# Two mixers in one fused kernel: VectorE's order in the triangular solve and in its setup, one identity copy cut in four, and the hg items spread 2 2 2 2 4 4 over the levels

## The reference, cut to what matters

```
p = h @ w_in                                  # 6672 columns, in weight pieces of 256
qkv, z, beta, a, hq, hf_fwd, hf_bwd, hi, hgate, gate_dn, gate_hg = split(p)
q, k, v = silu(conv5(qkv));  q, k = l2norm(q), l2norm(k)
# gated delta rule, forward and backward, 4 heads of 128:
A = strict_tril(beta * (k @ k.T) * decay);  T = inverse(I + A)
o_dn = (q k^T * decay) applied through T to beta * v
# HGRN2, forward and backward, 4 heads of 128:
logf = log_sigmoid(f) + log1p(lb * exp(-f));  kk = (1 - lb) * sigmoid(-f)
o_hg = sum over s <= t of (q_t . kk_s * exp(b_t - b_s)) * i_s,  b = cumsum(logf)
out = (sigmoid(gate_dn) * norm(o_dn) @ w1 + sigmoid(gate_hg) * norm(o_hg) @ w2) @ w_out
```

## Time and profile before

| | us |
|---|---|
| three runs | 1750.78, 1748.83, 1751.04 |
| median | 1750.78 |
| the profiled execution | 1750.08 |
| its span | 1748.3 |
| PE busy | 1655.1 (95%) |
| DVE busy | 1237.5 (71%) |
| ACT busy | 967.5 (55%) |

### The profile page before, as it was taken

The page is one execution under the profiler, slowest core; times in us unless marked ns, Lnnn a source line. Parts: engine busy times, 40 slices in busy tenths (PEclk is TensorE's granted clock), DMA queues, the critical chain, the costliest instruction groups (busy, mean ns, idle before and its releaser), DMA issues.

```text
span 1748.3 us, 30663 instructions
## 1 busy us (share of the span) xinstructions
PE 1655.1 (95%) x13206; PEld 1603.1 (92%) x13206; DVE 1237.5 (71%) x1715; ACT 967.5 (55%) x1420; POOL 0.2 (0%) x4
## 2 busy tenths in 40 slices
PE   6997899999999997899999998999999998899997
PEld 6987899999999897899999997887999998799997
DVE  6778955777747779846777747666688838688863
ACT  6564465565536663465556534347577635577752
POOL 0000000000000000000000000000000000000000
PEclk9999999999999999999999999999999999999999
DMA  6421115455454421124455552530354553054551
GB/s 256 168 97 49 49 40 181 164 197 190 172 191 138 178 73 49 49 73 169 167 195 193 178 185 90 199 120 1 120 194 173 190 193 127 25 193 173 189 193 49
DMA packets 34983, 246.11 MB, mean 141 GB/s; under 512 B 3872, under 2 KB 4256, under 8 KB 5536
## 3 DMA queue, kind: packets, MB, share of 16 engines
q1 hardware_dynamic: 34848, 244.15, 39.4%
HBM read 243.09 MB, written 1.05 MB: 140 GB/s over the span
## 4 chain that ended last, share of the span: by engine, by line
PE 80%; DVE 13%; ACT 5%; issue 1%; DMA 0%; DVEq 0%; ACTq 0%
PE PS L395 79%; DVE SA L1659 3%; DVE WL L1659 2%; ACT SB L1079 2%; DVE SB L1659 2%; DVE SB L1668 1%; ACT WH L1082 1%; DVE SB L1900 1%; ACT XH L1122 1%; PE PS L398 1%; DVE SB L1904 1%; DVE X L1659 1%; DVE SB L1663 0%; ACT SB L1082 0%; DVE SA L1851 0%
## 5 line engine op out<-in xcount | busy, mean ns | idle before, releaser
L395 PE MATMUL PS<-XH,WH 128*128 128x256 f32 (+1 forms) x2536 | 726.8, 287 | 18.0 <-DVE WL L1659 17.3
L395 PE MATMUL PS<-XL,WH 128*128 128x256 f32 (+1 forms) x2536 | 718.8, 283 | 0.0
L395 PE MATMUL PS<-XH,WL 128*128 128x256 f32 (+1 forms) x2536 | 718.6, 283 | 0.0
L1082 ACT CAST WH<-RAW 128x2048 fp32r<-128x2048 f32 (+1 forms) x226 | 426.4, 1887 | 470.9 <-PE PS L395 422.5
L1659 DVE TENSOR_TENSOR WL<-RAW,WH 128x2048 fp32r<-128x2048 f32 (+1 forms) x226 | 510.7, 2260 | 159.2 <-ACT WH L1082 149.3
L395 PEld LDWEIGHTS PS<-XH,WH 128*128 128x128 f32 (+1 forms) x2536 | 485.8, 192 | 22.3 <-issue 17.9
L395 PEld LDWEIGHTS PS<-XL,WH 128*128 128x128 f32 (+1 forms) x2536 | 485.9, 192 | 2.6 <-issue 1.9
L395 PEld LDWEIGHTS PS<-XH,WL 128*128 128x128 f32 (+1 forms) x2536 | 485.7, 192 | 0.3
L395 PE MATMUL PS<-INH,WH 128*128 128x256 f32 x960 | 268.9, 280 | 1.1 <-DVE INL L1659 1.1
L395 PE MATMUL PS<-INH,WL 128*128 128x256 f32 x960 | 269.7, 281 | 0.0
L395 PE MATMUL PS<-INL,WH 128*128 128x256 f32 x960 | 267.0, 278 | 0.0
(11 more groups left out here) (142 smaller groups left out, 1582.7 us busy)
## 6 DMA issues: line engine op xcount, KB each, us to landing
RAW<-w_in SPq DMA_DIRECT2D x52, 1024.0 KB, 4.8
RAW<-w_up SPq DMA_DIRECT2D x44, 1024.0 KB, 4.8
RAW<-f_in SPq DMA_DIRECT2D x44, 1024.0 KB, 4.9
RAW<-w_down SPq DMA_DIRECT2D x22, 1024.0 KB, 4.8
RAW<-f_out SPq DMA_DIRECT2D x22, 1024.0 KB, 4.9
RAW<-a_w_in SPq DMA_DIRECT2D x10, 1024.0 KB, 4.8
RAW<-w_out SPq DMA_DIRECT2D x8, 1024.0 KB, 5.0
RAW<-w_bdn SPq DMA_DIRECT2D x4, 1024.0 KB, 4.9
```

Source lines behind the costliest of these rows:

```text
L395: return e.matmul(out, l, r, start=start, stop=stop, skip_group_check=True)
L1082: e.copy(out, x).then_inc(*A.up(*key, of=of))
```

## The change

Eight things move; no arithmetic changes.

- `mixing` starts at b+16 instead of b+18, and `z_after` with it. Items 16 and 17 now use only two slots.
- The masks of mixer 0 are converted behind the hq projections instead of within the convolutions; PE's wait for them moves from "abT" to the rows.
- On ACT the `chunk()` that casts item 13 moves behind the eight l2/rq operations.
- On DVE `forget(0)` and both `unit` move ahead of a `chunk()`, gc and gB.
- The identity is copied in four quarters, each with its own count, and `dn_first` waits for its own quarter, not for the fence f2, which now stands ahead of "k sum".
- DVE's first `chunk()` of the solve stands behind `hg_exp(1)`, the second behind the first zproj.
- In each level zproj (the bank) comes before `hg_step`.
- The items are spread 2, 2, 2, 2, 4, 4.

```diff
-            mixing = [b for b in MIXERS if b + 18 <= i < b + 30]
+            mixing = [b for b in MIXERS if b + 16 <= i < b + 30]
-        z_after = [max(i for i in range(b + 18) if slot[i] == NRAW - 1) for b in MIXERS]
+        z_after = [max(i for i in range(b + 16) if slot[i] == NRAW - 1) for b in MIXERS]
+        HG_STEPS = (2, 2, 2, 2, 4, 4)
...
                     if c == 0:
-                        w.wait_ge(*V["masks"])
                         turned((st, "abT"), 16, abT, V["ab", st])
...
                         w.wait_ge(*V["gB", st])
+                        w.wait_ge(*V["masks"])
...
-                    n += 2
-                    if lv > 2:
-                        hg_mm(n)
-                        n += 1
+                    for m in range(2, HG_STEPS[lv - 1]):
+                        hg_mm(n + m)
+                    n += HG_STEPS[lv - 1]
...
                 act(nea, par("a_log", l * 8, 8), ACT.Exp, "nea", st)
-                chunk()
                 for n in (0, 2, 1, 3):
...
                     act(rq[:, sx], rq[:, sx], ACT.Exp, "rq", st, n, scale=-0.5)
+                chunk()
...
-                        cp(v3(XT, 16), ident.unsqueeze(1).to_broadcast([128, 16, 128]), "ident", st)
+                        for g4 in range(4):
+                            cp(XTv[:, g4], ident.unsqueeze(1).to_broadcast([128, 4, 128]), "ident", st, g4)
...
-                    if c == 4 and l == 0:
-                        masks()
...
                 if l == 0:
+                    masks()
                     lower_bounds()
...
                 ts(lb_, gw2[:, :, 0:8], -1.0, None, ALU.mult, None, "ln beta", st)
+                forget(0)
+                unit(0)
+                unit(1)
                 chunk()
                 w.wait_ge(*P["ps", st, "gc"])
                 cp(gc, v3(ps[st, "gc"][:, 0:16], 2), "gc", st, of=ps.out(st, "gc"))
...
-                forget(0)
-                unit(0)
-                unit(1)
                 rest(0)
...
-                waits(*f2)
...
-                    w.wait_ge(*A["ident", st])
+                    waits(A["ident", st, g4], V["at", st], A["f inv", st, 3])
...
-                chunk()
-                w.wait_ge(*V["k out", st, 3])
+                waits(V["k out", st, 3], *f2)
                 tt(ZR[2], kk_[:, 0:1024], kk_[:, 1024:2048], ALU.add, "k sum", st)
                 hg_exp(0)
                 hg_exp(1)
+                chunk()
                 hg_mul(0)
...
-                chunk()
                 w.wait_ge(*V["w lo", z_after[l]])
                 n = 0
                 for lv in range(1, 7):
-                    hg_step(n)
                     if lv < 5:
                         zproj(lv - 1)
+                    if lv == 1:
+                        chunk()
+                    hg_step(n)
...
-                    n += 2
-                    if lv > 2:
-                        hg_step(n)
-                        n += 1
+                    for m in range(2, HG_STEPS[lv - 1]):
+                        hg_step(n + m)
+                    n += HG_STEPS[lv - 1]
```

More of the change, by code:

```diff
@@ L1298, in mixer @@
                     dn_z(3, lv)
-                    n += 2
-                    if lv > 2:
-                        hg_mm(n)
-                        hg_exp(n + 2)
-                        n += 1
+                    for m in range(2, HG_STEPS[lv - 1]):
+                        hg_mm(n + m)
+                        hg_exp(n + m + 2)
+                    n += HG_STEPS[lv - 1]
                     if lv < 4:
@@ L1808, in mixer @@
                 if l == 0:
+                    masks()
                     lower_bounds()
                 chunk()
[L1811 to L1827, removed]
-                chunk()
[L1829 to L1832, removed]
-                waits(V["g", st], *f0, *(P["ps", st, "l2", n] for n in range(4)))
-                for j in range(2):
-                    cp(gB[:, j], g_[:, j, :].unsqueeze(2).to_broadcast([128, 8, 128]), "gB", st)
-                e.memset(bb[:, :, 0:1], 0.0).then_inc(*V.up("bb0", st))
                 def forget(c):
@@ L1865, in unit @@
                     tt(k_[:, sx], k_[:, sx], rq[:, sk], ALU.mult, "k", st, n)
+                pv = v3(ps[st, "abT"][:, 0:32], 2)
+                dtb = par("dt_bias", l * 8, 8).unsqueeze(1).to_broadcast([128, 2, 8])
+                waits(P["ps", st, "abT"], *f0)
+                ts(gw2[:, :, 0:8], pv[:, :, 0:8], -1.0, None, ALU.mult, None, "g in", st, of=ps.out(st, "abT"))
+                tt(gw2[:, :, 8:16], pv[:, :, 8:16], dtb, ALU.add, "g in", st, of=ps.out(st, "abT"))
+                w.wait_ge(*V["g in", st])
+                ts(gw1, gw2, -1.0, None, ALU.mult, None, "g neg", st)
+                w.wait_ge(*V["g neg", st])
+                tt(gw1, gw1, gw2, ALU.min, "g min", st)
+                w.wait_ge(*A["g ln", st])
+                stt(gw2, gw2, 0.0, gw1, ALU.max, ALU.add, "g sp", st)
+                w.wait_ge(*A["nea", st])
+                ts(nea, nea, -1.0, None, ALU.mult, None, "g nea", st)
+                w.wait_ge(*V["g nea", st])
+                w.wait_ge(*V["g sp", st])
+                tt(g_, gw2[:, :, 8:16], nea.unsqueeze(1).to_broadcast([128, 2, 8]), ALU.mult, "g", st)
+                ts(lb_, gw2[:, :, 0:8], -1.0, None, ALU.mult, None, "ln beta", st)
                 forget(0)
@@ L1869, in mixer @@
                 unit(1)
+                chunk()
+                w.wait_ge(*P["ps", st, "gc"])
+                cp(gc, v3(ps[st, "gc"][:, 0:16], 2), "gc", st, of=ps.out(st, "gc"))
+                waits(V["gc", st], V["ln beta", st])
+                tt(bg, lb_, gc, ALU.subtract, "bg", st)
+                waits(V["g", st], *f0, *(P["ps", st, "l2", n] for n in range(4)))
+                for j in range(2):
+                    cp(gB[:, j], g_[:, j, :].unsqueeze(2).to_broadcast([128, 8, 128]), "gB", st)
+                e.memset(bb[:, :, 0:1], 0.0).then_inc(*V.up("bb0", st))
                 rest(0)
```

## The result

| | before | after |
|---|---|---|
| median of the runs, us | 1750.91 | 1758.98 |
| lowest to highest of four | 1748.83 to 1751.43 | 1757.52 to 1761.78 |
| profiled execution | 1750.08 | 1757.52 |
| its span | 1748.3 | 1755.7 |

The changed kernel is slower by a ratio of 1.005, 95% interval 1.0033 to 1.0068. The forecast was 1755.0 in a range of 1749 to 1760. The work done is the same, and the page of the profile agrees with the earlier trace rows: DVE is busy for the same time, PE for 3.4 us less, in a span 7.4 us longer.

A forecast was written before the change was run, and what follows sets the result against it. The prediction took PE (95% busy) as the bound outside the mixers and a chain alternating between engines inside them; 2x3.4 + 0.2 - 2.4 = +4.6 us on 1750.08 gave 1754.7, stated as 1755.0, range 1749 to 1760.

The forecast's parts named there:

- the forecast's own line: Total time: the main case among the listed outcomes, 1753 to 1758 us, chance 0.48.
- The load behind WL 16: Solve: item 18's load waits for WL 16, its cast holds PE's first y until 669.35, 14.8 us idle.
- Rival 1: Solve: the load does not bite, being issued or landed before ACT gets there; 14.6 us faster, 1736; chance 0.08.
- Setup, mixer 1: Mixer 1 before row 0: k wait replaced by a 3.4 us bank wait, clock falls again; row 0 0.2 us later.
- Setup, mixer 0: Mixer 0 before row 0: masks leave the convolutions, no clock fall behind the remaining wait; row 0 2.4 us earlier.
- The bank waits: Solve: PE's 6.7 us of waits for a bank, 3.73 and 3.00, go because zproj comes first.
- walk along DVE: Solve: DVE's work followed level by level to PE's last hg matmul at 757.1 against 753.71, 3.4 us later.
- The solve: Each mixer, through the last hg matmul: 3.4 us later, bounds 1.7 and 4.2.
- the half clock behind the long wait: Solve, y and diagonal after PE's idle time: half clock costs 1.7 to 1.9 us, at most 2.4.
- The count of DVE's idle time: Solve cross-check: DVE idle 18.0 us against 14.9 before, so 3.1 us later.
- From mixer to mixer and behind the last hg matmul: Stretches between the mixers and after the last one: no term in the sum, 0 us.
- Rival 2: Solve: stall there but given back, no clock fall behind it; 1752.0 us, down to 1750; chance 0.31.

The follow-up runs named there:

- x1_slots: Kernel before with only the slot edit (items 16 and 17 limited to two RAW slots): 1764.73 us, ratio 1.008.
- x10_noslot: Changed kernel without the slot edit, item 17's low part placed ahead of zproj(0): 1739.03 us, ratio 0.9936.
- x2_cast: Changed kernel with ACT's cast of item 18 moved behind the hg exponent of item 2 in level 1: 1737.52 us, ratio 0.9927.
- x4_masks: Changed kernel with mixer 0's masks put back behind the fifth convolution: 1760.41 us, ratio 1.0059.
- x9_bank: x2_cast with zproj (the bank) moved back behind hg_step in all levels: 1738.84 us, ratio 0.9936.
- x6_steps: Changed kernel with the hg items spread 2 2 3 3 3 3 as before: 1758.11 us, ratio 1.0044.
- x5_ident: Changed kernel with the identity copied whole again and fence f2 ahead of the first placing: 1764.86 us, ratio 1.0085.
- x3_gb: Changed kernel with item 12's low part on DVE moved behind gc, bg and gB: 1750.72 us, ratio 1.0005.
- x11: x10_noslot with item 12's low part moved behind gc, bg and gB: 1728.96 us, ratio 0.9879.
- x12: Changed kernel with 110 added identity matmuls on PE between zproj(0) and the first y: 1773.23 us, ratio 1.0132.
- x8: x2_cast with item 12's low part behind gc, bg and gB, and the spread 2 2 3 3 3 3: 1731.66 us, ratio 0.9896.
- x7: x2_cast with item 12's low part moved behind gc, bg and gB: 1732.39 us, ratio 0.9898.

## Why the prediction was right, and which term was off

The mechanism came out as forecast, and the size less well. The profiled execution was forecast 4.6 us longer and was 7.4 longer, and the median of 1758.98 lies outside the 1753 to 1758 of the forecast's own line, 1 us inside the range. Of the 4.0 us above 1755.0, 2.7 are the two solves, -0.7 the two setups, 0.8 what no term stood for (-1.7 and +2.5), and 1.2 the median, which lies 1.5 above the profiled execution, for the 0.3 that 1755.0 allowed. That -1.7 and +2.5 nearly cancel is luck.

- **The load behind WL 16: as forecast.** Issue 662.46 (forecast 662.45), cast 667.37 (667.3), first y 669.41 (669.35), idle 14.9 (14.8). x1_slots and x10_noslot tie it to the slots, x2_cast to ACT's order. Rival 1 is out. The rule of the Trainium skill that the prediction weighed here (DMA: Bandwidth & Descriptors, Rules for kernel authors: issue early, wait late) holds in both directions: x10_noslot issues early, x2_cast waits late, and either is worth some 20 us.
- **Setup, mixer 1: as forecast.** gc at 610.13 in the chain, to the hundredth; resumption 610.27 (610.45) after 3.0 us; a half clock again for 3.4 us. Net -0.1 for +0.2.
- **Setup, mixer 0: as forecast.** The wait at ab 0.26 (0.3), no fall behind it, gc 88.6, resumption 88.73 (88.9). Net -2.8 for -2.4. x4_masks shows wait and fall come back together.
- **The bank waits: right that they go.** The one before zproj(3) stays away when the order or the spread is put back by itself (x9_bank, x6_steps). But the 6.7 us of them in the earlier trace rows were worth little: in x9_bank 4 us more of such a wait in each mixer cost 1.2 us each. The prediction had this in its walk along DVE, where the wait saved comes up again as waits for SA.
- **The solve: mis-sized, +3.4 forecast, +4.6 and +4.9 measured.** The term that was off is the half clock behind the long wait. I took 1.7 us, from 3.4 us of half clock, and at most 2.4. Measured: y and diagonal 8.50 us, 5.54 at full clock, so 2.96. That is 1.3 us a mixer of the 1.2 and 1.5 missing. Forecast 676.7 for the diagonal's end, measured 677.9. The rule of the Trainium skill that idle PE before matmuls makes them run cold (TensorE: Matmul & The Clock Gate, Loop structure matters more than you think) names a DMA wait, and this was one: the trace agrees, at 0.50. The bound of 2.4 rested on a misreading. The 4.7 us that I called the longest stretch of half clock with PE busy were not the longest: the trace of the kernel before has 6.80 us, in this window (columns as in the earlier trace rows).

```profile
1167.10:1173.90 6.80, 6.80 (x22) 4.85 (x22) 2.79 (x5) 4.02 (x18) 0.00 (x0) 0.50 0.00 0
```

  By the working of the prediction that is a cost of 3.4 us, and a bound that holds the 2.96. The length of the wait is no better guide. The changed kernel and the five others with this wait had it in both mixers, 14.3 to 17.8 us long, and the half clock behind the first y lasted 2.9 to 6.1 us: in x5_ident 6.1 in one mixer and 3.3 in the other, both after 17.8 us. Where it was short, more of it came later. The count of DVE's idle time is off in the same direction: 18.0 forecast, 19.75 measured. The time from the first y to the last hg matmul came to 89.2 us (forecast 87.8, before 97.0).
- **From mixer to mixer and behind the last hg matmul: not forecast.** I had zero in both places. They came to -1.7 and +2.5, and the unedited rest of the program is what lifts the profiled execution from 1755.0, where 4.9 at the last hg matmul would leave it, to 1757.5. The half-clock windows lie elsewhere in the two kernels: before has one at 542 that after lacks, after has one at 1068 and one at 1187.
- **Rival 2 (no clock fall, the stall given back), at 0.31, had its condition nowhere:** a fall stood behind the 15 us wait in both mixers of each of the five kernels besides the changed one that had the wait and no filler.

The stretch behind the last hg matmul is the same code in all of these kernels. Its length in their profiles goes by how much half clock lay in it (the window at the very end left out, which every kernel has):

| half clock, us | length of the stretch, us |
|---|---|
| 13.1 to 13.7 | x11 993.3, x3 993.7, x6 994.2 |
| 17.1 | before 994.6, x1 994.7, x9 994.8, x12 995.3, x8 995.7, x2 995.9 |
| 20.1 to 20.5 | x10 996.7, x5 996.8, x4 997.1, after 997.1, x7 997.3 |

It spans 4.0 us with no edit at all, in no order of the time at which it starts, and the three groups do not overlap. That the half clock causes it is thus well supported, but not shown: no experiment here moved these windows alone.

## What to carry to other kernels

When a buffer's rotation changes, find the last reader of the former item and look at what now stands ahead of it on its own engine, and then at what stands behind the first user of the new item: here a load of 4.8 us became a wait of 14.9, because a low part stood behind 9 us of DVE work and PE's first product counted a cast that it did not need. Price the clock behind a wait as a range, with the longest stretch of half clock in the whole trace as its bound (6.80 us here), and count the half clock up to the end of the edited stretch: what does not come behind the wait can come later in it. And judge an edit at the last instruction of the code that it touches before reading the total, since here the total carried up to 4 us from code that nobody edited.

## What the runs showed that I had not expected

- A wait of 14.9 us left PE at half clock for 6.1 us of work (5.5 in mixer 0), where waits of 3.2 and 2.1 us had 3.4 behind them.
- In x3_gb the same wait of 15 us, begun 1.9 us earlier, had only 2.9 us of half clock behind it (656.8 to 670.5, first y at 667.54), and the time to the last hg matmul was still 88.8 us against 89.2, since two further falls came at 742.1 and 755.8.
- Ten runs of x3_gb spread over 11.8 us (1746.79 to 1758.56), the other experiments over 1.2 to 5.5.
